# Moving the sample's input-projection stage into the interleaved back phase of the prompt

## What is computed

```python
def mixer(h, h0_fwd, h0_bwd, p):
    z = h @ p["w_in"]
    xr, yr, u, v = jnp.split(z, 4, axis=-1)          # 512 columns each
    xc = dw_conv(xr, p["lru_conv_w"], p["lru_conv_b"], LRU_CONV_LEFT)
    hf = rglru_direction(xc, h0_fwd, ..., False)     # gated scan, forward
    hb = rglru_direction(xc, h0_bwd, ..., True)      # gated scan, backward
    o_lru = jax.nn.gelu(yr) * (hf + hb)
    s = einsum over 128-position chunks of gelu(v) + bias
    o_sgu = gelu(u) * s
    o = concatenate([rms_norm(o_lru, ...), rms_norm(o_sgu, ...)])
    return o @ p["w_out"], hf[:, -1], hb[:, 0]

def layer(x, mod, ...):
    h = rms_norm(x, norm1) * (1 + sc1) + sh1
    x = x + g1 * mixer(h)
    h = rms_norm(x, norm2) * (1 + sc2) + sh2
    x = x + g2 * conv_ffn(h)                         # up, width-3 conv, silu gate, down
```

## Time and profile before

| | us |
|---|---|
| median of 3 runs (lowest, highest) | 905.61 (904.2, 905.87) |
| the profiled execution, its own time | 903.59 |
| its span on the slowest core (core 2) | 902.1 |
| spans of the eight cores | 893.9 to 902.1 |
| TensorE busy with matmuls, core 2 | 649.1 (72%) |
| VectorE busy | 604.8 (67%) |
| ScalarE busy | 405.4 (45%) |
| GpSimd busy (it only issues weight loads) | 95.9 (11%) |

### The profile page before, as it was taken

One profiled execution on the slowest core, in us unless ns is written; L12 is line 12 of the kernel. 1 busy time (PEld: TensorE's weight loads), 2 busy tenths in 40 slices (PEclk: granted clock), 3 DMA queues, 4 the chain that ended last, 5 costly groups with the idle time before them and its releaser, 6 DMA issues.

```text
span 902.1 us, 10885 instructions; the slowest of 8 cores (893.9 to 902.1 us)
## 1 busy us (share of the span) xinstructions
PE 649.1 (72%) x3080; PEld 281.2 (31%) x3080; DVE 604.8 (67%) x912; ACT 405.4 (45%) x611; POOL 95.9 (11%) x184
## 2 busy tenths in 40 slices
PE   0235423888567999764359697999799588999793
PEld 0112210335122443221124432444244433443341
DVE  3047764663788999888977346999674337999512
ACT  1206724343465555544374436555625436555203
POOL 2102110001000111000001000111111000111110
PEclk9956565889687999886569878999999888999997
DMA  8599899236243997532029964997599974997572
GB/s 164 110 158 157 142 209 248 90 112 117 48 70 49 148 155 124 87 62 44 1 37 161 208 167 74 153 150 129 80 140 167 206 172 77 151 153 126 90 121 93
DMA packets 37851, 111.64 MB, mean 124 GB/s; under 512 B 3361, under 2 KB 3617, under 8 KB 37794
## 3 DMA queue, kind: packets, MB, share of 16 engines
q0 software_dynamic: 25920, 87.70, 60.1%
q1 hardware_dynamic: 11874, 23.26, 8.0%
HBM read 192.33 MB, written 6.30 MB: 220 GB/s over the span
## 4 chain that ended last, share of the span: by engine, by line
PE 49%; DVE 26%; issue 8%; DMA 8%; ACT 6%; DVEq 1%; SPq 0%; ACTq 0%
PE psum_all L218 49%; DVE sb_S L229 17%; DMA sb_S<-xp 4%; DMA sb_S<-xs 3%; ACT sb_H L226 2%; DVE sb_S L233 2%; ACT sb_S L226 1%; DVE sb_A L490 1%; ACT psum_all L226 1%; DMA sb_wring<-wada 1%; DVE sb_H L229 1%; ACT L226 1%; DVE sb_H L237 1%; DVE sb_S L494 1%; DVEq L112 1%
## 5 line engine op out<-in xcount | busy, mean ns | idle before, releaser
L218 PE MATMUL psum_all<-sb_H,sb_wring 128*128 128x512 bf16 x2272 | 547.3, 400 | 57.3 <-ACT sb_H L226 17.6
L218 PEld LDWEIGHTS psum_all<-sb_H,sb_wring 128*128 128x128 bf16 x2272 | 228.1, 101 | 373.6 <-issue 140.7
L229 DVE SCALAR_TENSOR_TENSOR sb_S<-psum_all,sb_pp,sb_S 128x504 f32<-128x504 f32 (+1 forms) x288 | 207.5, 741 | 22.6 <-ACT sb_S L226 6.5
L226 ACT ACTIVATE sb_H<-sb_S 128x512 bf16<-128x512 f32 x112 | 64.0, 621 | 190.5 <-PE psum_all L218 70.7
L218 PE MATMUL psum_all<-sb_H,sb_ones_bf 128*128 128x512 bf16 x112 | 43.4, 456 | 94.1 <-ACT sb_H L226 91.8
L226 ACT ACTIVATE sb_S<-psum_all,sb_pp 128x512 f32<-128x512 f32 x144 | 104.0, 766 | 9.2 <-PE psum_all L218 8.9
L226 ACT ACTIVATE sb_S<-sb_S 128x512 f32<-128x512 f32 x72 | 45.4, 630 | 123.3 <-DVE sb_S L229 123.3
L229 DVE SCALAR_TENSOR_TENSOR sb_S<-psum_all,sb_modT,sb_S 128x512 f32<-128x512 f32 x48 | 35.4, 748 | 64.5 <-PE psum_all L218 61.3
L218 PE MATMUL psum_all<-sb_H,sb_gw 128*128 128x512 bf16 x64 | 27.6, 559 | 69.7 <-DVE sb_H L440 26.8
L253 POOL DMA_DIRECT2D sb_wring<-wup x72 | 38.2, 530 | 313.3 <-PE psum_all L218 313.3
L229 DVE SCALAR_TENSOR_TENSOR sb_S<-sb_A,sb_pp,sb_S 128x512 f32<-128x512 f32 x80 | 60.1, 751 | 8.4
(11 more groups left out here) (58 smaller groups left out, 373.0 us busy)
## 6 DMA issues: line engine op xcount, KB each, us to landing
sb_wring<-wup POOLq DMA_DIRECT2D x72, 512.0 KB, 6.7
sb_wring<-wdn POOLq DMA_DIRECT2D x48, 384.0 KB, 5.5
sb_wring<-wada POOLq DMA_DIRECT2D x24, 512.0 KB, 14.6
sb_S<-xs SPq DMA_DIRECT2D x6, 2048.0 KB, 9.5
sb_wring<-win POOLq DMA_DIRECT2D x22, 512.0 KB, 9.2
sb_wring<-wout POOLq DMA_DIRECT2D x12, 512.0 KB, 7.9
sb_S<-xp SPq DMA_DIRECT2D x2, 2048.0 KB, 21.8
ys<-sb_S SPq DMA_DIRECT2D x2, 2048.0 KB, 15.8
```

The source lines that it names most:

```text
L218: P.op("pe", lambda e: e.matmul(out, lhsT=lhsT, rhs=rhs, start=start, stop=stop), reads, writes)
L226: P.op("act", lambda e: e.activation(out=out, in_=in_, func=func, **kw), reads, writes)
L229: P.op("dve", lambda e: e.scalar_tensor_tensor(out=out, in0=in0, scalar=scalar, in1=in1, op0=op0, op1=op1), reads, writes)
```

## The change

The loop at L727 to L741 goes. In its place a generator `sample_xr_side` emits the same work as five side steps: one that only loads the first two x tiles, then one for each tile with front, part a, part b and the load of the next tile into the same buffer. The side of the prompt's `phase_b2` is now this generator followed by `sample_front`, and the rate after an untagged yield is 2 instead of 1. The x buffers are LR and XC instead of XT and LR; the squares go to H slots 20 to 23; h of tiles 3 and 2 goes to XCB. `xr_back_a` is called without slots, so each tile asks for its two units of weights again.

```diff
-    HX = 16
-    XT2 = LR
-    plan = [(3, XT, HX), (2, XT2, HX), (0, XT, HK), (1, XT2, HK + 8)]
-    rbs = {}
-    xslots = [wload(win_d[0], 2048), wload(win_d[1], 2048)]
-    for i in range(2):
-        t, xb, hs_ = plan[i]
-        rbs[t] = xr_front(xs_d, t * T, xb, SQ + 4 * (i % 2), 4)
-    for i in range(4):
-        t, xb, hs_ = plan[i]
-        bks = xr_back_a(xb, rbs[t], 0, hs_, xslots)
-        if i + 2 < 4:
-            t2, xb2, _ = plan[i + 2]
-            rbs[t2] = xr_front(xs_d, t2 * T, xb2, SQ + 4 * (i % 2), 4)
-        xr_back_b(bks, [t], [(0, T, 2 + t * T)])
+    def sample_xr_side():
+        bufs = [LR, XC]
+        order = [3, 2, 0, 1]
+        hsl = {3: XCB, 2: XCB, 0: HK, 1: HK + 8}
+        load_x(xs_d, order[0] * T, bufs[0])
+        load_x(xs_d, order[1] * T, bufs[1])
+        yield
+        for i, t in enumerate(order):
+            xb = bufs[i % 2]
+            rb = norm_front(xb, HID + 20, 4)
+            bks = xr_back_a(xb, rb, 0, hsl[t])
+            xr_back_b(bks, [t], [(0, T, 2 + t * T)])
+            if i + 2 < 4:
+                load_x(xs_d, order[i + 2] * T, xb)
+            yield
+
+    def side_all():
+        yield from sample_xr_side()
+        yield from sample_front()
...
-    interleave(phase_b2(xp_d, 0, True, H2, 1, 256, yp_d, 0), sample_front(), {None: 1.0, "f": 0.0, "d": 6.0})
+    interleave(phase_b2(xp_d, 0, True, H2, 1, 256, yp_d, 0), side_all(), {None: 2.0, "f": 0.0, "d": 6.0})
```

## The result

The changed kernel takes 957.69 us, the median of 8 runs (956.8 to 959.52), against 905.13 for the kernel before in 8 runs of the same comparison: a ratio of 1.0588, 95% interval 1.0575 to 1.0601. It is 5.9% slower; the medians differ by 52.6 us. Forecast were 957, between 937 and 977. In some executions of any of these kernels the cores of one half of the chip show a lower granted clock and need some per cent longer; the ratios leave these out. The profiled execution took 959.52, its span on the slowest core, core 1, is 958.0. In this part core 1 stands some 0.8 us behind the times shown of core 2 before.

A forecast was written before the change was run, and what follows sets the result against it. VectorE sets the pace from 235.5 on, with idle time only before (28.4 and 19.7 us). 903.6 plus 67.3 late at the up-projection minus 14.3 given back makes 956.6; forecast 957, range 937 to 977.

The forecast's parts named there:

- part 2: One sample tile's serial chain of norm, pairs and matmuls, nothing overlapping: 24.7 us, 26.0 with a table load.
- rival B: Start and clock worse: weight loads delay tile 3 up to 6.8 us, clock 3 us a tile; 970 to 980, 13%.
- part 1: Start of the sample's xr work: tile 3 lands at 153.25; the other tiles' loads are not waited for.
- part 3: Tile chains, v projection and SGU in sequence: first output residual at about 272.5, before at 239.98.
- part 4: Output-projection stage: 78.1 us, including 4 for the second norm's wait; up-projection reached 67.3 us late.
- part 5: Down-projection: moved side steps give time back; last gates plus 96 matmuls make it 92.9 us, 14.3 shorter.
- if TensorE could run ahead: Down-projection: the stage would be 22 us shorter instead of 14.3, the low end.
- "d": Down-projection stage with its side steps: 14.3 us shorter, uncertain by -8 to +2.
- Rivals C to E: Chains partly overlap, about 930, 9%; work fills norm waits, 877, 5%; VectorE's work only moves, 904 to 906, 3%.
- the signs named as wrong: Next tile's squares before the last copy; gaps on weight landing; down-projection at 85; an xr tile every 16 us.
- those named as right: Include first output residual near 272, large landing wait ending at 153, up-projection from about 350, clock 0.50 in gaps.
- The two rules: Trainium skill: table switches add a 1.38 drain, not adopted; DMA engines take turns between queues, left to rival B.

The follow-up runs named there:

- the repaired kernel: Changed kernel with tile 3 in XT and each tile's front emitted between part a and part b of the tile before; ratio 1.0185, median 924.95 us.

## Why the prediction was right, point by point

**The direction and the main mechanism (part 2)** are shown. A tile's chain was put at 24.7 us, 26.0 with a table load. On core 1 the four took, from first square to the end of the last copy, 27.2 (162.78 to 189.98), 27.3 (196.58 to 223.93), 24.8 and 25.3. The chains by themselves cost 28.9 us in the kernel before; pipelining takes 13.5 of the changed kernel's loss away. The term for the matmuls and the last copy behind the pairs, put at 8.1 us, was 9.3, 8.9, 8.2 and 8.9, at granted clocks of 0.71, 0.70, 0.77 and 0.71 where the row had 0.79: slower by 0.1 to 1.2 us, not by rival B's 3.

**The start (part 1)** was mis-sized. Landing was taken from a row of a kernel in which no weight load was issued during the transfer; 162.78 came for 153.25, 8 us later on the cores' mean, and holding the two weight loads brings back 7. It was in rival B as a possibility with the right cause. The other half of rival B, v and the tiles wholly at the lower clock, did not come: v's matmuls took 7.15 us at a granted clock of 1.00, as before. That the late first chain is a term of its own was in the walk, but not priced: it is 22 us, the 7 included.

**The walk (part 3)** gave the first output residual at 272.5; it came at 283.2 on core 1. 9.5 of the 10.7 are the landing, 2.5 the longer chains of tiles 3 and 2, and the SGU took 1 us less (247.73 to 256.79 is 9.1 against 10.2); what is left are tenths in the v projection and in tile 1.

**The output-projection stage (part 4)** was put at 78.1 us and took 75.1. The wait for the second norm, taken as 4, was 0.77:

```profile
345.22 0.43 DVE L440 CAST sb_H<-sb_S 128x512 bf16<-128x512 f32 x1
346.42 1.41 DVE L229 SCALAR_TENSOR_TENSOR sb_S<-sb_S,sb_w,psum_all 128x512 f32<-128x512 f32 x2 [0.77 <-ACT psum_all L226]
```

The gates' activations on ScalarE, feared to delay the squares, had ended at 338.9, and the Exp ended at 346.3, 0.7 us behind VectorE's last conv step. A wait of 1.05 us for TensorE ahead of the up-projection (358.28) was not in the sum.

**The down-projection (part 5)** was put at 92.9 and took 84.7, the value named as its low end. TensorE in time:

```profile
505.33 6.18 PE L218 MATMUL psum_all<-sb_H,sb_wring 128*128 128x512 bf16 x24
...
515.53 20.88 PE L218 MATMUL psum_all<-sb_H,sb_wring 128*128 128x512 bf16 x96 [1.16 <-ACT sb_S L226]
```

The 96 matmuls took 20.88, 0.218 each, not the 0.25 of the earlier trace rows: the granted clock was 1.00 in their stretch, but 0.87 in that of the 72 and 0.50 ahead of it (461.0 to 465.8). That is 3.1 of the 8.2 us. The other 5.1 are the start: VectorE's side work ended 83.6 us into the stage, just as computed, but the prediction set the last gates' matmuls at the place of VectorE's last gate step, and TensorE had them done before; that is the case "if TensorE could run ahead", named as the low end. Core 1, TensorE's last gate matmul and VectorE's last pair of gate products:

```profile
513.99 0.38 PE L218 MATMUL psum_all<-sb_H,sb_gw 128*128 128x512 bf16 x1 [0.20 <-ACT sb_S L226]
520.36 1.28 DVE L233 TENSOR_TENSOR sb_S<-sb_S 128x512 f32<-128x512 f32 x2
```

The 96 end at 536.4, and VectorE's side work at 535.3. The tail doesn't stand out here, while it does by 10 us with five tiles.

**The sum.** 67.3 late at the up-projection was 75.0 (cores' mean, 355.1 - 280.1), 14.3 given back was 22.2 (75.0 - 52.8). Two errors of some 8 us with opposite signs, so that the total fits better than its terms: with one of them alone it would have been some 965 or 949, still inside the range, but the hit to 1 us is luck. Nor did every term stay inside its own bounds: the landing came 7.9 late on the cores' mean (bound +6.8), and "d" was 8.2 shorter than put (bound -8). Rivals C to E are out by their times (930, 877, 904), and B by its total (970 to 980). Of the signs named as wrong one did show, "d" at 85. Of those named as right, the one long landing wait is there, but ends at 162.8 and not at 153, and the first residual came at 283 and not near 272; the granted clock from a tile's first statistics to its last pair was 0.50 to 0.61. Behind the final norm, where nothing different was forecast, the two profiled executions differ by 3.1 us on the cores' mean (416.0 and 412.9); that was not taken apart.

**The two rules.** The row held against the first, a drain with each switch of tables: Ln begins 0.02 us after the table load's end (201.64 + 1.28 and 202.94), and 20 ns is no drain. Nor is it hidden ahead of the load: ScalarE stood 0.81 us ahead of it, and 0.83 ahead of tile 0's Ln, which needs no load. In the kernel with rate 2 alone (core 1) a load follows an activation at once:

```profile
314.18 1.38 ACT L226 ACTIVATE sb_H<-sb_S,sb_modT 128x512 bf16<-128x512 f32 x2 [0.29 <-DVE sb_S L229]
315.58 1.28 ACT L226 ACT_TABLE_LOAD   x1
316.88 0.69 ACT L226 ACTIVATE sb_S<-psum_all,sb_hba 128x512 f32<-128x512 f32 x1
```

The second rule held where the row misled: the Trainium skill, "DMA: Bandwidth & Descriptors", Queues, rings and completion order, says that an engine takes turns between queues, and the runs with held weights agree, 6.5 us earlier; "served by age" falls between queues, while within SyncE's queue the run with the second x load put off (0.6 us) doesn't speak against it.

What stays open: the last 8 us between the repaired kernel (18.8 over before) and the rate's 11.0. They weren't taken apart. A guess that no run shows: u, v and SGU then stand between xr tiles with no conv step beside them until the last tile.

## What to carry to other kernels

Merging two stages by generators changes the program order of every engine, and a coarse side step is a serial piece: it brings its own latency, and whatever the main stage does waits behind it, and the other way round. Before moving a stage, write down what its hand-made pipeline hides (29 us here), split it into steps at the points where one engine hands over to the next, and see that VectorE always has a ready step from elsewhere. Where the idle time of a sound order is a wait for data, look for free slots and ask earlier, and keep prefetches of weights that are needed much later from taking turns with it. Together with earlier conv steps that gave 2.6% here (6.3 us by the buffers, 8.0 by the conv steps, 9.5 by the held weights).

## What the runs showed of the hardware that was not expected

A 2 MB load of x on SyncE's queue wasn't served ahead of 512 KB weight loads that were issued later on GpSimd's: two that came 2 and 5 us after it made its first square 6.5 us later on the mean of eight cores. A second 2 MB load right behind it in the same queue cost it nothing that can be seen (0.6 us). And in the four-buffer kernel with early convs, keeping four weight loads out of the way moved tile 2's first square from 156.55 to 141.18 on core 1, and from 154.6 to 141.0 on the cores' mean. SyncE issued the first x load at 124.9 and at 123.2 on core 1, so the earlier place of the loads in the program explains at most 1.7 us of it.
